# Second half of a branch merge: fp32 products as three fp32r products, with the weights' low parts made on GpSimd

## The chip, the cores and the metric
One core of one Trainium2 chip runs the whole kernel. The metric is the device time of one execution in microseconds (us), the median over runs. fp32r is float32 rounded to fewer bits, for TensorE; a "high part" is a value rounded to fp32r, a "low part" is what is left of it.

## The reference, cut to what matters
One layer of a hybrid backbone over 1024 latent tokens, width 1024. What the change touches is the merge of two branches:

```
def _merge(y_a, y_b, gate_logits, w_branch_a, w_branch_b, w_out):
    ga, gb = jnp.split(jax.nn.sigmoid(gate_logits), 2, axis=-1)
    return (ga * (y_a @ w_branch_a) + gb * (y_b @ w_branch_b)) @ w_out
...
    x_new = x + g1 * _merge(y_a, y_b, zx[..., OFF_G:], w_branch_a, w_branch_b, w_out)
    hx2 = _rms(x_new, norm2) * (1 + sc2) + sh2
    x_new = x_new + g2 * _expert_choice(hx2, router, w_gate, w_up, w_down)
```

y_a (from a long convolution) and y_b (from attention) are 1024 tokens by 512; w_branch_a and w_branch_b are 512 by 1024, w_out is 1024 by 1024. Before the merge stand the input projection, the attention and the long convolution; behind it the router, the choice of 128 tokens by each of 16 experts, and the experts' three matrices.

## The kernel before, in words
The kernel is a row of stages, each a block in which every engine has its own list of instructions and waits on semaphores; between stages all engines meet. The merge (`merge`, L1732 to L2080) is one such stage.

It works on transposed data: channels on the 128 partitions, tokens along the free axis. The inputs lie in SBUF when the stage starts: ya, yb, wa and wb, four chunks of 128 rows each, loaded (all but ya) during the convolution stage by `load_merge_input` (L1509). Sixteen branch jobs follow (L1857 to L1865, `m` in the list of jobs of L1787): job i has the half of the tokens h = i // 8 and the output chunk j = i % 8. In the first half a job has four fp32 products of 128x128 by 128x512 (w_a by y_a only); the part of y_b was computed in the stage before and comes back from DRAM as `mb_dram`. In the second half a job has eight, four for each branch. PSUM holds four jobs; job i waits until VectorE has read the bank of job i-4 (`read`).

VectorE follows with `gated(i)` (L1978): the gate by the first product (one operand in PSUM), the gate by the second (in the first half both operands in SBUF), and their sum; ScalarE rounds the sum to mT_hi (L1918); VectorE subtracts to get mT_lo (`merged_low`, L1995). The gates come from DRAM, two jobs ahead, on SP's queue (L1814), and behind the first two SP issues the load of w_out, 4 MB (L1819). ScalarE makes w_out's high parts (`out_high`, L1908) in the second half of the jobs, VectorE its low parts (`out_low`, L1973): two in front of each of the last four gated jobs for the left half of the columns, and eight behind the last job for the right half.

Then the output projection: `project(t, n)` (L1842) takes 128 tokens and 512 columns and issues 24 fp32r matmuls (8 chunks by three products, `three`, L220: high by high, high by low, low by high). The order is project(0,0), project(1,0), project(0,1), then tile by tile with the transposes and router products between (L1866 to L1899). VectorE multiplies by g1 (L2021), adds x (L2024), and the norm follows. SP loads the tiles of x (L1826) and stores the new ones (L1833), and after w_out's last low part it loads the first expert weights (L1828 to L1830). GpSimd has one memset in this stage (L1969).

Places in SBUF are shared by hand: wo_hi lies where ya and yb lie, wo_lo where wa and wb lie; a high or low part of w_out is written only when the branch products have read what it overwrites.

Of the kernel before, what the change touches and what calls it, by code (L numbers as in the profile page):

```python
# [20 lines left out]
P = 128  # L21
D = 1024
# [111 lines left out]
def build(nc, A, out):  # L134
    root = ExitStack()
    with root:
# [56 lines left out]
        with ExitStack() as s:  # L193
            sby, _ = scope(s)

            with ExitStack() as below:
                sbw, _ = scope(below)
                g["wo_hi"], g["wo_lo"] = (sbw(n, [P, KD, D], F32R) for n in ("wo_hi", "wo_lo"))
            g["ya"] = sby("ya", [P, NCH, L])
            with ExitStack() as below:  # L200
                sbw, _ = scope(below)
                g["yb"], g["wa"], g["wb"] = (sbw(n, [P, NCH, D]) for n in ("yb_in", "w_a", "w_b"))
            hyena(g, right, filters)
            g["late"] = root.enter_context(nc.sbuf_tensor("late", [P, L], F32, side="right"))
            g["affT"] = g["late"][0:AFF, 0:L // 2]

            with ExitStack() as below:
                g["mT_hi"], g["mT_lo"] = (below.enter_context(nc.sbuf_tensor(n, [P, KD, L], F32R, side="right"))
                                          for n in ("mT_hi", "mT_lo"))
            g["ring"] = root.enter_context(nc.sbuf_tensor("ring", [P, RAW, 2048], F32, side="right"))  # L210
            g["raw_in"] = [sem(f"raw_in{i}") for i in range(RAW)]
            merge(g)
# [1241 lines left out]
def convolve(g, KS, ti):  # L1454
# [9 lines left out]
    with ExitStack() as s:  # L1464
# [29 lines left out]
        with nc.Block() as block:  # L1494
            @block.sync
            def _(sp):
                def load_columns(j):
                    if j >= 2:
                        sp.wait_ge(branch_done, j - 1)
                    sp.dma_start(w2[:, j % 2], A["w_branch_b"][0][:, P * j:P * j + P].rearrange("(c p) n -> p c n", p=P))\  # L1500
                      .then_inc(w2_in[j % 2], 16)

                def load_gate(i):
                    if i:
                        sp.wait_ge(gated, 2 * i)
                    at = HY * (i // 2 + 1) + HC * (i % 2)
                    sp.dma_start(gate[:], g["z_dram"][at:at + HC, :].rearrange("(c p) t -> p c t", p=P)).then_inc(gate_in, 16)

                def load_merge_input(i, tile, src):  # L1509
                    sp.wait_ge(spec_ready, 2 * FC * (i + 1))  # L1510
                    sp.dma_start(tile[:], src.rearrange("(c p) n -> p c n", p=P)).then_inc(g["merge_in"], 16)

                load_columns(0)
                load_columns(1)
                sp.dma_start(y2[:], g["yb_dram"][:, 0:512].rearrange("(c p) t -> p c t", p=P)).then_inc(y2_in, 16)
                load_gate(0)
                load_columns(2)
                load_columns(3)
                load_columns(4)
                load_gate(1)  # L1520
                load_columns(5)
                load_merge_input(0, g["yb"], g["yb_dram"])
                load_gate(2)
                load_columns(6)
                load_merge_input(1, g["wa"], A["w_branch_a"][0])
                load_gate(3)
                load_columns(7)
                load_merge_input(2, g["wb"], A["w_branch_b"][0])

            @block.tensor  # L1530
            def _(pe):
# [200 lines left out]
def merge(g):  # L1732
# [10 lines left out]
    ident, mod, A2, ring = g["ident"], g["mod"], g["A2"], g["ring"]  # L1743
    ya, yb, wa, wb = g["ya"], g["yb"], g["wa"], g["wb"]
    mT_hi, mT_lo, wo_hi, wo_lo = g["mT_hi"], g["mT_lo"], g["wo_hi"], g["wo_lo"]
    wo = ring[:, 0:4].rearrange("p s n -> p (s n)").rearrange("p (k n) -> p k n", n=D)
    XB = 2
    with ExitStack() as s:
        sb, ps = g["scope"](s)
        sb("merge_inputs", [P, 3, NCH, D])  # L1750
        x_new = sb("x_new", [P, XB, D])
        step = sb("m_step", [P, D])
        mb = step[:].rearrange("p (b n) -> p b n", b=2)
        xn = sb("x_normed", [P, 2, D])
# [16 lines left out]
        job, read = sem("m_job"), sem("m_read")  # L1771
        mul, mt_ready, mt_hi, mt_lo = sem("m_mul"), sem("mt_ready"), sem("mt_hi"), sem("mt_lo")
        wo_high, wo_low = sem("wo_hi_ready"), sem("wo_lo_ready")
        xnew_ready, sq_ready = sem("xnew_ready"), sem("sq2_ready")
        v_step, rt_ready, xn_ready = sem("v2_step"), sem("rt2_ready"), sem("xn2_ready")
        h_ready = sem("h2_ready")
# [30 lines left out]
        with nc.Block() as block:  # L1807
            @block.sync
            def _(sp):
                for i in range(M):  # L1810
                    if i >= 2:
                        sp.wait_ge(mt_ready, i - 1)
                    h, j = divmod(i, KD)
                    sp.dma_start(gates[:, i % 2], g["gate_dram"][:, half(h)]  # L1814
                                 .rearrange("(v c p) t -> c p v t", v=2, p=P)[j]).then_inc(gates_in[i % 2], 16)
                    if h == 0:
                        sp.dma_start(mb[:, i % 2], g["mb_dram"][P * j:P * j + P, :]).then_inc(mb_in[i % 2], 16)
                    if i == 1:
                        sp.dma_start(wo, A["w_out"][0].rearrange("(c p) n -> p c n", p=P)).then_inc(o_in, 16)  # L1819
                        sp.dma_start(router[:], A["router"][0].rearrange("(c p) n -> p c n", p=P)).then_inc(r_in, 16)  # L1820
                for t in range(NT):
                    if t >= XB:
                        sp.wait_ge(x_stored[t % XB], 16 * (t // XB))
                        sp.wait_ge(xn_ready, t - XB + 1)
                        sp.wait_ge(job, n_job[("h", t - XB)])
                    sp.dma_start(x_new[:, t % XB], A["x"][0, P * t:P * t + P, :]).then_inc(xr_in[t % XB], 16)  # L1826
                    if t == 1:
                        sp.wait_ge(wo_low, 2 * NO)  # L1828
                        for i in range(4):
                            load_unit(sp, g, 0, i)  # L1830
# [10 lines left out]
            def _(pe):  # L1841
                def project(t, n):  # L1842

                    if t % 4 == 0 and n == 0:
                        pe.wait_ge(mt_lo, KD * (t // 4 + 1))
                    if t == 0:
                        pe.wait_ge(wo_low, NO * (n + 1))
                    if n == 0:
                        pe.wait_ge(read, M + 2 * (t - 1) if t >= 2 else M - 2 + t)
                    for k in range(KD):  # L1850
                        at = slice(P * t, P * t + P)
                        mm = three(pe, pj[:, t % 2, n], mT_hi[:, k, at], mT_lo[:, k, at],
                                   wo_hi[:, k, half(n)], wo_lo[:, k, half(n)], k == 0, k == KD - 1)
                    return mm

                pe.wait_ge(g["merge_in"], 48)
                for kind, t in jobs:  # L1857
                    if kind == "m":
                        h, j = divmod(t, KD)
                        if t >= 4:  # L1860
                            pe.wait_ge(read, t - 3)
                        for br, (w, y) in enumerate(((wa, ya), (wb, yb))[:h + 1]):
                            for c in range(NCH):
                                mm = pe.matmul(pj[:, t % 4, br], w[:, c, P * j:P * j + P], y[:, c, half(h)],
                                               start=c == 0, stop=c == NCH - 1)  # L1865
                    elif kind == "o":  # L1866
                        if t == 0:
                            project(0, 0)
# [38 lines left out]
            def _(act):  # L1907
                def out_high(k, n):  # L1908
                    act.activation(wo_hi[:, k, half(n)], wo[:, k, half(n)], ACT.Copy).then_inc(wo_high, 1)

                for i in range(M):
                    h, j = divmod(i, KD)
                    if i >= KD:
                        act.wait_ge(o_in, 16)
                        act.wait_ge(job, KD)
                        out_high(i - KD, 0)
                    act.wait_ge(mt_ready, i + 1)
                    act.activation(mT_hi[:, j, half(h)], ta[:, i % 2], ACT.Copy).then_inc(mt_hi, 1)  # L1918
                act.wait_ge(job, M)
                for k in range(NO):  # L1920
                    out_high(k, 1)

# [44 lines left out]
            @block.gpsimd  # L1967
            def _(pool):
                pool.memset(aff[:], 0.0).then_inc(aff_zero, 1)  # L1969

            @block.vector
            def _(dve):
# [22 lines left out]
                def merged_low(i):  # L1995
# [2 lines left out]
                    dve.tensor_tensor(mT_lo[:, j, half(h)], ta[:, i % 2], mT_hi[:, j, half(h)].bitcast(F32), ALU.subtract)\  # L1998
                       .then_inc(mt_lo, 1)

                for i in range(M):
                    if i >= KD + 4:
                        for k in range(2):
                            dve.wait_ge(job, KD + 4)
                            out_low(2 * (i - KD - 4) + k, 0)
                    gated(i)
                    merged_low(i)
                for k in range(NO):
                    out_low(k, 1)
# [442 lines left out]
```

## Time and profile before
| | us |
|---|---|
| median of 3 runs | 2245.38 |
| lowest and highest | 2242.11, 2246.43 |
| profiled execution, span from first to last instruction | 2242.3 |
| TensorE busy | 2145.9 (96%) |
| VectorE busy | 1655.7 (74%) |
| ScalarE busy | 1147.0 (51%) |
| GpSimd busy | 175.8 (8%) |

The profiled execution has its span on record, and no whole time of its own beside it; the median of the runs is 3.1 us longer than this span. PE is TensorE's matrix multiplication, PEld its weight load, DVE is VectorE, ACT ScalarE, POOL GpSimd, SP the engine that issues most DMAs (SPq its queue). TensorE's matmuls are pipelined, so the length of one record is more than the distance to the next; the pace is read from counts over a stretch. An fp32 matmul of 128x512 is two records. PEclk is the granted clock as a share of 2.4 GHz.

### The profile page before, as it was taken

The page shows a single profiled execution, that of the slowest core. Times are in us where ns is not written, and L with a number is a line of the kernel's source. Part 1 is how long each engine was busy: PE and PEld are TensorE (multiplying, and loading weights), DVE is VectorE, ACT ScalarE, POOL GpSimd, SP SyncE. Part 2 cuts the span into 40 slices and gives each one's busy share as a digit, 9 for nine tenths or more (in the row PEclk, how much of TensorE's full clock was granted, in tenths as well). Part 3 has the DMA queues.
Part 4 walks back from the last instruction along what each step waited for, and adds up shares of the span by engine and source line. Part 5 has one row for each costly group of instructions (what it writes and reads, how often), then busy time and mean ns, then how long its engine had stood idle before and what let it go on. Part 6 is the DMA issues. An engine that isn't in the chain of part 4 may idle for free.

```text
span 2242.3 us, 27253 instructions
## 1 busy us (share of the span) xinstructions
PE 2145.9 (96%) x10057; PEld 1695.6 (76%) x10057; DVE 1655.7 (74%) x1707; ACT 1147.0 (51%) x1201; POOL 175.8 (8%) x53
## 2 busy tenths in 40 slices
PE   7999999989999999999489999999999999999998
PEld 2998888856567776468468888888888888888886
DVE  3668754167654897553688889889889989898986
ACT  3521212165500220121257777777777777777775
POOL 0000000010000000000011011111011111011100
PEclk9999999999999999999789999999999999999999
DMA  8134454130020232643569999999999999999993
GB/s 305 61 98 163 142 178 141 47 118 13 17 80 6 70 131 91 221 168 113 197 236 364 393 394 380 380 378 380 399 391 380 378 382 384 396 387 380 380 378 121
DMA packets 183291, 539.38 MB, mean 241 GB/s; under 512 B 15231, under 2 KB 57355, under 8 KB 182708
## 3 DMA queue, kind: packets, MB, share of 16 engines
q1 hardware_dynamic: 172768, 506.72, 60.3%
q0 software_dynamic: 4752, 16.78, 2.9%
q10 hardware_dynamic: 5700, 14.90, 1.7%
q8 instruction: 48, 0.79, 0.1%
q14 instruction: 23, 0.19, 0.0%
HBM read 502.71 MB, written 35.65 MB: 240 GB/s over the span
## 4 chain that ended last, share of the span: by engine, by line
PE 49%; DVE 2%; DMA 0%; issue 0%; ACT 0%; POOL 0%; POOLq 0%
PE p_y L222 5%; PE p_y L224 5%; PE p_a L222 5%; PE p_a L224 5%; PE p_y L223 5%; PE p_a L223 5%; PE p_b L224 5%; PE p_b L223 5%; PE p_b L222 5%; PE p_t L2350 1%; PE p_t L2341 1%; DVE idx_rows L2305 1%; DVE late L2308 0%; DVE vals L2303 0%; DMA g1row<-xn_dram,idx_e 0%
## 5 line engine op out<-in xcount | busy, mean ns | idle before, releaser
L2246 DVE TENSOR_TENSOR r_lo<-ring,r_hi 128x2048 fp32r<-128x2048 f32 x384 | 865.8, 2287 | 62.8 <-ACT r_hi L2205 56.0
L2205 ACT ACTIVATE r_hi<-ring 128x2048 fp32r<-128x2048 f32 x384 | 731.0, 1915 | 154.4 <-PE p_b L224 74.7
L222 PE MATMUL p_y<-r_hi,a_hi 128*128 128x512 f32 x512 | 205.3, 401 | 0.0
L222 PE MATMUL p_a<-r_hi,x_hi 128*128 128x512 f32 x512 | 202.5, 396 | 1.0 <-DVE x_lo L2257 1.0
L224 PE MATMUL p_y<-r_hi,a_lo 128*128 128x512 f32 x512 | 200.0, 391 | 0.0
L224 PE MATMUL p_a<-r_hi,x_lo 128*128 128x512 f32 x512 | 199.8, 390 | 0.0
L223 PE MATMUL p_a<-r_lo,x_hi 128*128 128x512 f32 x512 | 199.2, 389 | 0.0
L223 PE MATMUL p_y<-r_lo,a_hi 128*128 128x512 f32 x512 | 199.2, 389 | 0.0
L222 PE MATMUL p_b<-r_hi,x_hi 128*128 128x512 f32 x512 | 199.2, 389 | 0.0
L223 PE MATMUL p_b<-r_lo,x_hi 128*128 128x512 f32 x512 | 199.2, 389 | 0.0
L224 PE MATMUL p_b<-r_hi,x_lo 128*128 128x512 f32 x512 | 199.2, 389 | 0.0
L222 PE MATMUL p_z<-h_hi,w_hi 128*128 128x512 f32 x448 | 177.0, 395 | 0.0
L224 PE MATMUL p_z<-h_hi,w_lo 128*128 128x512 f32 x448 | 174.5, 390 | 0.0
L223 PE MATMUL p_z<-h_lo,w_hi 128*128 128x512 f32 x448 | 174.4, 389 | 0.0
L2168 POOL DMA_INDIRECT g1row<-xn_dram,idx_e x16 | 121.4, 7587 | 58.5 <-issue 43.3
L2174 POOL DMA_INDIRECT out_x<-late,idx_s x17 | 45.3, 2666 | 914.6 <-DVE late L2296 914.6
L224 PEld LDWEIGHTS p_y<-r_hi,a_lo 128*128 128x128 f32 x512 | 96.1, 188 | 21.0
L224 PEld LDWEIGHTS p_a<-r_hi,x_lo 128*128 128x128 f32 x512 | 96.1, 188 | 20.5
L222 PEld LDWEIGHTS p_a<-r_hi,x_hi 128*128 128x128 f32 x512 | 96.2, 188 | 20.2 <-issue 1.4
L223 PEld LDWEIGHTS p_b<-r_lo,x_hi 128*128 128x128 f32 x512 | 96.1, 188 | 20.0
L222 PEld LDWEIGHTS p_b<-r_hi,x_hi 128*128 128x128 f32 x512 | 96.1, 188 | 20.0
L224 PEld LDWEIGHTS p_b<-r_hi,x_lo 128*128 128x128 f32 x512 | 96.1, 188 | 19.9
(319 smaller groups left out, 3577.7 us busy)
## 6 DMA issues: line engine op xcount, KB each, us to landing
ring<-in_w_gate SPq DMA_DIRECT2D x128, 1024.0 KB, 8.4
ring<-in_w_up SPq DMA_DIRECT2D x128, 1024.0 KB, 8.5
ring<-in_w_down SPq DMA_DIRECT2D x128, 1024.0 KB, 12.0
w_raw<-in_w_in SPq DMA_DIRECT2D x17, 1024.0 KB, 6.1
ada_rest<-in_ada_w SPq DMA_DIRECT2D x16, 1024.0 KB, 5.3
ada<-in_ada_w SPq DMA_DIRECT2D x8, 1024.0 KB, 15.3
gate_dram<-zs ACTq DMA_DIRECT2D x16, 512.0 KB, 2.6
x_normed<-gate_dram SPq DMA_DIRECT2D x16, 512.0 KB, 4.3
```

The source lines that it names most:

```text
L222: pe.matmul(out, a_hi, b_hi, start=start, stop=False)
L223: pe.matmul(out, a_hi, b_lo, start=False, stop=False)
L224: return pe.matmul(out, a_lo, b_hi, start=False, stop=stop)
L2168: pool.indirect_dma_start(out=xe[:], out_offset=None, in_=g["xn2_dram"][:, :], in_offset=bass.IndirectOffsetOnAxis(ap=idx_e[:, 0:1], axis=0))\
L2174: pool.indirect_dma_start(out=rows, in_=part, in_offset=None, out_offset=bass.IndirectOffsetOnAxis(ap=idx_s[:, at:at + 1], axis=0), comput ...
L2205: act.activation(r_hi[:, i % PARTS], ring[:, i % RAW], ACT.Copy).then_inc(hi_ready, 1)
L2246: dve.tensor_tensor(r_lo[:, i % PARTS], ring[:, i % RAW], r_hi[:, i % PARTS].bitcast(F32), ALU.subtract).then_inc(lo_ready, 1)
L2305: dve.max_index(rows[:, at], vals[:, at], aff).then_inc(found, 1)
L2341: mm = pe.transpose(p_t[:, bank, P * k:P * k + P], xe[:, P * (4 * q + k):P * (4 * q + k) + P], ident[:])
L2350: mm = pe.transpose(p_t[:, q % 2, P * k:P * k + P], au[:, q % 2, P * k:P * k + P], ident[:])
```

## The change
It does the branch products of the second half of the tokens (jobs 8 to 15) as three fp32r products each, as the projection does. The first half stays in fp32.

ScalarE makes the high parts of y_a and y_b for tokens 512 to 1023 (8 copies at the start of the stage) and those of the weights (two copies ahead of each of the first eight waits for mt_ready). VectorE makes the low parts of y (8 subtractions ahead of gated(0)). GpSimd makes the low parts of the weights (16 subtractions of 128x512, each after its high part; the one of w_a also after the first-half job that reads the same columns). Low parts lie in the place of the values they come from. The high parts lie where the second half of mT_hi and mT_lo will be (weights), where x_new will be (y_a), and in `late` and the unused first half of yb (y_b). So four things move: x is loaded after job 15; chunks 6 and 7 of w_out's left high parts are made after job 15; w_out's left low parts go behind `gated` in place of ahead of it; and the projection waits for them chunk by chunk. The convolution stage loads only the second half of y_b's tokens.

```
@@ load_merge_input, in the convolution stage @@
-                load_merge_input(0, g["yb"], g["yb_dram"])
+                load_merge_input(0, g["yb"][:, :, 512:L], g["yb_dram"][:, 512:L])
@@ merge: places @@
+    wa_hi, wb_hi = ([m[:, j, 512:L].rearrange("p (c n) -> p c n", c=NCH) for j in range(KD)] for m in (mT_hi, mT_lo))
+    wa_lo, wb_lo = g["wa_lo"], g["wb_lo"]
+        ya_lo = [g["ya_r"][:, c, second] for c in range(NCH)]
+        yb_lo = [g["yb_r"][:, c, second] for c in range(NCH)]
+        ya_hi = [x_parts[:, c] for c in range(NCH)]
+        yb_hi = [g["late_r"][:, 0], g["late_r"][:, 1], g["yb_r"][:, 2, 0:512], g["yb_r"][:, 3, 0:512]]
@@ sync @@
+                sp.wait_ge(job, M)
                 for t in range(NT):
@@ tensor, project @@
-                    if t == 0:
-                        pe.wait_ge(wo_low, NO * (n + 1))
+                    if t == 0 and n:
+                        pe.wait_ge(wo_low, 2 * NO)
                     for k in range(KD):
+                        if t == 0 and n == 0 and k in (0, 6, 7):
+                            pe.wait_ge(wo_low, max(k + 1, 6))
@@ tensor, branch jobs @@
-                        for br, (w, y) in enumerate(((wa, ya), (wb, yb))[:h + 1]):
+                        column = slice(P * j, P * j + P)
+                        for c in range(NCH if h == 0 else 0):
+                            mm = pe.matmul(pj[:, t % 4, 0], wa[:, c, column], ya[:, c, half(0)],
+                                           start=c == 0, stop=c == NCH - 1)
+                        branches = ((wa_hi[j], wa_lo, ya_hi, ya_lo), (wb_hi[j], wb_lo, yb_hi, yb_lo))
+                        for br, (w_hi, w_lo, y_hi, y_lo) in enumerate(branches if h else ()):
+                            if j == 0:
+                                pe.wait_ge(y_low, NCH * (br + 1))
+                            pe.wait_ge(w_low, 2 * j + br + 1)
                             for c in range(NCH):
-                                mm = pe.matmul(pj[:, t % 4, br], w[:, c, P * j:P * j + P], y[:, c, half(h)],
-                                               start=c == 0, stop=c == NCH - 1)
+                                mm = three(pe, pj[:, t % 4, br], w_hi[:, c], w_lo[:, c, column], y_hi[c], y_lo[c],
+                                           c == 0, c == NCH - 1)
@@ scalar @@
+                act.wait_ge(g["merge_in"], 48)
+                for y, y_hi in ((ya, ya_hi), (yb, yb_hi)):
+                    for c in range(NCH):
+                        act.activation(y_hi[c], y[:, c, second], ACT.Copy).then_inc(y_high, 1)
                 for i in range(M):
                     h, j = divmod(i, KD)
-                    if i >= KD:
+                    if i < KD:
+                        for w, w_hi in ((wa, wa_hi), (wb, wb_hi)):
+                            act.activation(w_hi[i], w[:, :, P * i:P * i + P], ACT.Copy).then_inc(w_high, 1)
+                    elif i < M - 2:
                         act.wait_ge(o_in, 16)
                         act.wait_ge(job, KD)
                         out_high(i - KD, 0)
+                    elif i == M - 1:
+                        act.wait_ge(job, M)
+                        out_high(6, 0)
+                        out_high(7, 0)
@@ gpsimd @@
+                for n in range(2 * KD):
+                    j, br = divmod(n, 2)
+                    w, w_hi, w_lo = ((wa, wa_hi, wa_lo), (wb, wb_hi, wb_lo))[br]
+                    column = slice(P * j, P * j + P)
+                    pool.wait_ge(w_high, n + 1)
+                    if br == 0:
+                        pool.wait_ge(job, j + 1)
+                    pool.tensor_tensor(w_lo[:, :, column], w[:, :, column], w_hi[j].bitcast(F32), ALU.subtract)\
+                        .then_inc(w_low, 1)
@@ vector @@
+                for b, (y, y_hi, y_lo) in enumerate(((ya, ya_hi, ya_lo), (yb, yb_hi, yb_lo))):
+                    for c in range(NCH):
+                        dve.wait_ge(y_high, NCH * b + c + 1)
+                        dve.tensor_tensor(y_lo[c], y[:, c, second], y_hi[c].bitcast(F32), ALU.subtract).then_inc(y_low, 1)
                 for i in range(M):
+                    gated(i)
                     if i >= KD + 4:
                         for k in range(2):
-                            dve.wait_ge(job, KD + 4)
                             out_low(2 * (i - KD - 4) + k, 0)
-                    gated(i)
                     merged_low(i)
```

## Rows read from the trace of the kernel before

**Rows 1.** The page, its first part: busy time of each engine.
```profile
PE 2145.9 (96%) x10057; PEld 1695.6 (76%) x10057; DVE 1655.7 (74%) x1707; ACT 1147.0 (51%) x1201; POOL 175.8 (8%) x53
```

**Rows 2.** Merge by stretches: first half, second half, projection's start; busy us (x instructions).
```profile
core 0: us, PE busy (x) PEld busy (x) DVE busy (x) ACT busy (x) POOL busy (x), PEclk, DMA share, GB/s
892.43:921.15 28.72, 28.68 (x63) 12.72 (x64) 12.20 (x19) 2.52 (x4) 0.26 (x1) 0.94 0.85 302
921.15:976.11 54.96, 54.96 (x130) 24.32 (x129) 32.13 (x50) 11.09 (x19) 0.00 (x0) 1.00 0.40 130
976.11:992.93 16.82, 16.82 (x73) 13.39 (x72) 7.69 (x13) 4.80 (x9) 0.00 (x0) 1.00 0.39 148
```

**Rows 3.** Branch products by tile p_m: ns min/median/max, first and last start.
```profile
L1864 PE MATMUL p_m<-ya,w_a x128: 592/592/1193, 892.5 to 972.7; 128*128 128x512 f32 x128
L1864 PE MATMUL p_m<-yb_in,w_b x64: 592/592/593, 925.0 to 976.1; 128*128 128x512 f32 x64
```

**Rows 4.** Timeline of the first half's end: start us, us, what.
```profile
897.77 0.69 DVE L1984 TENSOR_TENSOR h<-x_normed,p_m 128x512 f32<-128x512 f32 x1 [5.83 <-PE p_m L1864]
...
899.88 7.34 SPq L1814 DMA_DIRECT2D x_normed<-gate_dram  x1
...
912.55 0.69 DVE L1984 TENSOR_TENSOR h<-x_normed,p_m 128x512 f32<-128x512 f32 x1 [7.88 <-DMA x_normed<-gate_dram]
...
916.03 0.68 DVE L1984 TENSOR_TENSOR h<-x_normed,p_m 128x512 f32<-128x512 f32 x1
916.63 0.69 DVE L1990 TENSOR_TENSOR h<-x_normed,m_step 128x512 f32<-128x512 f32 x1
...
919.41 0.68 DVE L1984 TENSOR_TENSOR h<-x_normed,p_m 128x512 f32<-128x512 f32 x1
920.01 0.69 DVE L1990 TENSOR_TENSOR h<-x_normed,m_step 128x512 f32<-128x512 f32 x1
...
924.61 0.19 PEld L1864 LDWEIGHTS p_m<-yb_in,w_b 128*128 128x128 f32 x1 [0.24 <-issue]
...
932.98 0.68 DVE L1984 TENSOR_TENSOR h<-x_normed,p_m 128x512 f32<-128x512 f32 x1
```

**Rows 5.** Copies and subtractions of w_out: eight in a row, and the groups' means.
```profile
979.38 4.26 ACT L1909 ACTIVATE wo_hi<-ring 128x512 fp32r<-128x512 f32 x8
...
980.12 4.90 DVE L1975 TENSOR_TENSOR wo_lo<-ring,wo_hi 128x512 fp32r<-128x512 f32 x8
...
L1918 ACT ACTIVATE mT_hi<-h 128x512 fp32r<-128x512 f32 x16 | 10.1, 629 | 84.5 <-DVE h L1993 84.5
L1909 ACT ACTIVATE wo_hi<-ring 128x512 fp32r<-128x512 f32 x16 | 9.2, 616 | 0.0
```

**Rows 6.** GpSimd's two-input operation, by its line: ns min/median/max.
```profile
L974 POOL TENSOR_TENSOR fpm<-fout x2: 2349/2362/2375, 463.3 to 465.6; 128x1024 f32<-128x1024 f32 x2
```

**Rows 7.** GpSimd's indirect DMAs and VectorE's subtractions in the expert stage.
```profile
1135.13 1.14 POOL L2168 DMA_INDIRECT g1row<-xn_dram,idx_e  x1 [39.06 <-issue]
...
L2168 POOL DMA_INDIRECT g1row<-xn_dram,idx_e x16: 1141/7957/8845, 1135.1 to 2105.8; - x16
...
L2246 DVE TENSOR_TENSOR r_lo<-ring,r_hi x384: 2278/2285/2295, 1139.7 to 2223.9; 128x2048 fp32r<-128x2048 f32 x192
```

**Rows 8.** Timeline of the hand-over to the projection.
```profile
976.11 0.19 PEld L222 LDWEIGHTS p_m<-wo_hi,mT_hi 128*128 128x128 f32 x1 [0.24 <-issue]
...
984.93 0.29 DVE L2012 TENSOR_TENSOR router_scaled<-router_w,A 128x128 f32<-128x128 f32 x1
```

**Rows 9.** Loads of x on SP's queue, their time to landing, and the first use.
```profile
965.51 0.94 SPq L1826 DMA_DIRECT2D x_new<-in_x  x2
...
x_new<-in_x SPq DMA_DIRECT2D x8, 512.0 KB, 4.5
...
993.53 0.69 DVE L2021 TENSOR_TENSOR m_step<-p_m,g1row 128x512 f32<-128x512 f32 x1 [8.31 <-PE p_m L224]
```

**Rows 10.** Stretches around the clock's dip and in the choice of tokens; columns as rows 2.
```profile
896.00:900.00 4.00, 4.00 (x11) 1.75 (x10) 1.98 (x3) 0.11 (x1) 0.00 (x0) 1.00 0.92 342
...
1014.00:1018.00 4.00, 4.00 (x20) 3.52 (x20) 2.18 (x10) 2.00 (x5) 0.00 (x0) 0.64 0.32 33
1018.00:1022.00 4.00, 4.00 (x17) 3.20 (x17) 0.00 (x0) 0.00 (x0) 0.00 (x0) 0.93 0.91 356
...
1100.00:1110.00 10.00, 0.00 (x0) 0.00 (x0) 9.52 (x23) 0.95 (x1) 0.00 (x0) 0.50 1.03 415
```

More of the change, by code:

```diff
@@ L198, in build @@
                 g["wo_hi"], g["wo_lo"] = (sbw(n, [P, KD, D], F32R) for n in ("wo_hi", "wo_lo"))
+            with ExitStack() as below:
+                sbw, _ = scope(below)
+                g["ya_r"], g["yb_r"], g["wa_lo"], g["wb_lo"] = (sbw(n, [P, NCH, D], F32R)
+                                                                for n in ("ya_parts", "yb_parts", "w_a_lo", "w_b_lo"))
             g["ya"] = sby("ya", [P, NCH, L])
@@ L203, in build @@
             hyena(g, right, filters)
+            with ExitStack() as below:
+                g["late_r"] = below.enter_context(nc.sbuf_tensor("late_parts", [P, 2, L // 2], F32R, side="right"))
             g["late"] = root.enter_context(nc.sbuf_tensor("late", [P, L], F32, side="right"))
@@ L1510, in load_merge_input @@
                     sp.wait_ge(spec_ready, 2 * FC * (i + 1))
-                    sp.dma_start(tile[:], src.rearrange("(c p) n -> p c n", p=P)).then_inc(g["merge_in"], 16)
+                    sp.dma_start(tile, src.rearrange("(c p) n -> p c n", p=P)).then_inc(g["merge_in"], 16)
                 load_columns(0)
@@ L1521, in _ @@
                 load_columns(5)
-                load_merge_input(0, g["yb"], g["yb_dram"])
+                load_merge_input(0, g["yb"][:, :, 512:L], g["yb_dram"][:, 512:L])
                 load_gate(2)
                 load_columns(6)
-                load_merge_input(1, g["wa"], A["w_branch_a"][0])
+                load_merge_input(1, g["wa"][:], A["w_branch_a"][0])
                 load_gate(3)
                 load_columns(7)
-                load_merge_input(2, g["wb"], A["w_branch_b"][0])
+                load_merge_input(2, g["wb"][:], A["w_branch_b"][0])
             @block.tensor
@@ L1750, in merge @@
         sb("merge_inputs", [P, 3, NCH, D])
+        with ExitStack() as below:
+            x_parts = g["scope"](below)[0]("x_parts", [P, NCH, 512], F32R)
         x_new = sb("x_new", [P, XB, D])
+        second = slice(512, L)
+        ya_lo = [g["ya_r"][:, c, second] for c in range(NCH)]
+        yb_lo = [g["yb_r"][:, c, second] for c in range(NCH)]
+        ya_hi = [x_parts[:, c] for c in range(NCH)]
+        yb_hi = [g["late_r"][:, 0], g["late_r"][:, 1], g["yb_r"][:, 2, 0:512], g["yb_r"][:, 3, 0:512]]
         step = sb("m_step", [P, D])
@@ L1773, in merge @@
         wo_high, wo_low = sem("wo_hi_ready"), sem("wo_lo_ready")
+        y_high, y_low = sem("y_hi_ready"), sem("y_lo_ready")
+        w_high, w_low = sem("branch_hi_ready"), sem("branch_lo_ready")
         xnew_ready, sq_ready = sem("xnew_ready"), sem("sq2_ready")
@@ L1916, in _ @@
                         out_high(i - KD, 0)
+                    elif i == M - 1:
+                        act.wait_ge(job, M)
+                        out_high(6, 0)
+                        out_high(7, 0)
                     act.wait_ge(mt_ready, i + 1)
                     act.activation(mT_hi[:, j, half(h)], ta[:, i % 2], ACT.Copy).then_inc(mt_hi, 1)
-                act.wait_ge(job, M)
                 for k in range(NO):
```

## The prediction

> **What bounds the kernel now.** I read the engine totals first, then the merge in stretches, then VectorE's order of time inside it, and last the places where the end of the merge is handed on. TensorE is busy 96% of the span [rows 1], so the first question is what its own work in the changed stage costs. The sixteen branch jobs run without a gap: eight for the first half of the tokens (four fp32 products each), eight for the second half (eight each), and then the output projection [rows 2]. Each fp32 product is two matmul records, 128 records for w_a and 64 for w_b [rows 3]. The second half takes 54.96 us for 128 records, 0.429 us a record and 0.859 us a product; in the projection 72 fp32r matmuls take 16.82 us, 0.2336 us each, and three of them 0.701 us [rows 2].
>
> VectorE has room in the second half (32.1 us of 55) but not in the first. There it waits for gates that stand behind the 4 MB load of w_out: the gates of job 2, due at 899.88, take 7.34 us to be issued, and gated(2) starts at 912.55. From then one job costs VectorE 3.38 us (916.03 to 919.41), as much as TensorE's 3.43 us for four products [rows 4]. TensorE has four banks, so job i needs the second multiply of gated(i-4). Job 8, the first of the second half, begins 8 records before the load at 924.61, at 921.18; the multiply that frees its bank starts at 920.01 and is out by 920.7. So the margin is some 0.45 us there, and by the same rows as little at jobs 6 and 7.
>
> **The change, part by part.** The range of my sum hangs on two terms, the products and what GpSimd does to VectorE.
>
> *Products.* 64 products at 0.859 - 0.701 = 0.158 us: 10.1 us less on TensorE. It has no gap there, so all of it is on the path if nothing else becomes late. A second-half job falls from 6.87 to 5.61 us. The first half keeps its fp32 form.
>
> *High parts on ScalarE.* Eight copies of y (0.53 us each at the pace of eight like copies in a row, 0.62 for one alone [rows 5]) start with the stage and end some 4.3 to 5 us later. The sixteen of w go in pairs ahead of each wait for mt_ready, 1.2 us in a cycle of 3.4 in which ScalarE now has one copy of 0.63 us. They are hidden by VectorE's three operations on the next job; without that cover they would cost 1.2 us a cycle.
>
> *Low parts of y on VectorE.* Eight subtractions, paced at 0.61 us like those of w_out [rows 5], end near 892.4 + 0.6 + 8 x 0.61 = 897.9 us, and gated(0) started at 897.77 [rows 4]. Behind them waits the whole job loop, but gated(2) waits for its gates until 912.55 in any case. Nothing. If the gates came early, it would cost at most 5 us of a lead that TensorE's four banks half hide.
>
> *Low parts of w on GpSimd.* The nearest row is a two-input operation on 128x1024 in 2.36 us [rows 6]; for 128x512 the bounds are 1.18 us (half the elements) and 2.36 us (no gain from the smaller size). I take 1.2: two of them in a row leave almost no fixed part between them. Sixteen are 19 us, spread over TensorE's first 29 us; the last pair may start when job 7 is done (921.2) and is needed by job 15 near 960. So GpSimd is not late by itself. What counts is what it does beside VectorE. In this trace no VectorE operation with two SBUF inputs stands beside a GpSimd one that reads SBUF. The nearest rows are the indirect DMAs: 1.14 us for the one issued while VectorE idled, 7.96 us in the median beside the back-to-back r_lo subtractions, which keep their 2.28 to 2.30 us [rows 7]. So the two engines can hold each other up, and bounds for VectorE are nothing (as r_lo) and the whole of GpSimd's time. I take the whole, less what falls beside VectorE's waits and its first multiply, which reads PSUM and one SBUF tile. Per job: 2 x 1.2 = 2.4 us, less 0.6 for the first multiply and 0.1 of gaps, 1.7 us more. The Trainium skill, SBUF — State Buffer, section Who interferes with whom, says so in words: an operation of VectorE with two SBUF inputs and a GpSimd operation that reads SBUF exclude each other, and the later one stands still until the earlier has ended. By that rule the sum is the one I give; by the r_lo row alone it would be 10.1 us. No run here shows that pair yet.
>
> Where it falls: w_hi of job j is made after mT_hi of job j-1, so GpSimd's pair for j = 0 to 2 is over before 912.55, and those for j = 3 to 7 run beside gated(3) to gated(7). The pair for job 3 starts near 915.95, and gated(3)'s second multiply (916.63) is held to 917.15 or 918.35, as GpSimd's second operation goes behind it or before it. Job 7 of TensorE waits up to 1.3 us, and job 8 waits for gated(4)'s: 920.7 + 1.7 + 0.5 to 1.7 = 922.9 to 924.1 against 921.18, so 1.7 to 2.9 us, and I take 2.3. Job 9 needs gated(5)'s by 924.1 + 3.4 + 0.5 to 1.7 = 928.0 to 929.2 and comes at 928.5 to 929.7: TensorE at 5.61 us a job now outruns the delay. VectorE falls back 5 x 1.7 = 8.5 us by gated(8) (932.98 before, 941.5 after [rows 4]), then takes 3.4 us a job, and from gated(12) some 4.0 (the wait for ScalarE is now covered by the two w_out subtractions), 967.0 for gated(15): TensorE ends job 15 at 921.18 + 2.3 + 44.9 = 968.4. It has caught up, by a little over 1 us.
>
> *Hand-over.* Two of the w_out low parts now stand after gated(15), for their place holds y_b's high part. Before, the last subtraction ended 8.9 us after the projection began (976.11, and 984.93 for the operation behind it [rows 8]). Now it is 1.25 us more behind that job, less 0.65 of wait covered: 9.5 us. The first 48 matmuls of the projection cover 11.2 us, so 1.7 us are left and the cost is nothing; uncovered it would be 1 us. The first wait of the projection, six low parts, is met by gated(14)'s pair, near 966.
>
> *Loads of x.* They move behind job 15 on SP's queue, because their place holds y_a's high part. Before, both were issued at 965.51 and used at 993.53 + 0.7 [rows 9]; now they go near 968.4 and land 4.5 us later, while the first use is 17 us off. Behind them on SP stands the expert weights' first load, which waits for the last w_out low part anyway. Nothing. The halved load of y_b (1 MB less) lies far ahead in the Hyena stage: nothing.
>
> *Clock.* The granted clock is 1.00 from 896 on, with a dip to 0.64 and 0.93 in 1014 to 1022, right after the small router matmuls [rows 10]. At 0.36 x 4 + 0.07 x 4 = 1.7 us it is the size of what a shifted start can gain or lose; I take nothing and keep 1.7 us both ways. Later, TensorE idles through the choice of the experts' tokens (0 us of 10 in 1100 to 1110 [rows 10]), so all behind the merge shifts whole.
>
> Sum: -10.1 + 2.3 = -7.8 us. Against the profiled execution's span of 2242.3 that is 2234.5; 3.1 us lie between the span and the median of the three runs, 2245.38, which gives 2237.6.
>
> **Rivals.** *No interference.* If VectorE is not held at all, TensorE keeps its 10.1 us: 2235.3. For it: r_lo's unchanged length. Against it: the sevenfold indirect DMA. A short lock, shared in another order, lies between this and my case.
>
> *GpSimd holds VectorE until it is the bound.* With c us more per job, VectorE frees job 11's bank at 930.9 + 5c, and five jobs of 5.61 us later the projection begins at 959 + 5c. It equals 976.1 at c = 3.4, that is at 2.05 us per GpSimd operation. With the upper bound of 2.36 us, c is 4.0: 979, 3 us slower, 2248.3; with a clock dip more, 2250. For it: the strided columns of w, which no row has. Against it: two back-to-back operations of 1024 elements at 2.35 and 2.37 show little that would not shrink with the size.
>
> *A middle case.* c = 2.7 (1.7 us per operation) gives 972.5, a gain of 3.6: 2241.8, inside the 0.2% (4.5 us) that a measurement of this kernel can tell from no change.
>
> *The products do not get cheaper.* If three fp32r matmuls cost here what one fp32 product does (0.286 us a matmul), nothing is gained and the 2.3 us of delay stay: 2247.7. Nothing in rows 2 speaks for it: the same shapes with the same weight loads run at 0.2336.
>
> **How the numbers follow.** My case 0.50, no interference 0.22, the middle case 0.14, GpSimd as the bound 0.10, no cheaper products 0.04. The forecast is my case, 2237.6. The range reaches to the no-interference case with a gain of the clock, 2233.6, and up over the middle case to 2243.0. Faster by over 0.2% means below 2240.9: my case and the first rival, 0.72; within it the middle case and half of the last two, 0.21, since 2247.7 and 2248.3 lie within 4.5 us of the median; slower by more, with the clock against it, their other half, 0.07.
>
> **What would show it.** Right: 192 records of fp32r matmuls at 0.2336 us in the second half, w_lo operations near 1.2 us or stretched, VectorE's second multiply or add of jobs 3 to 7 longer or late by about 1.7 us a job, job 8 some 2 us after its granted time and no wait of TensorE after it. Wrong: w_lo above 2 us, a projection that begins later than 971 or that stops before its third run of 24, a wait on the last w_out low part, or a dip of the clock elsewhere.

## The result and the profile after

The changed kernel takes 2233.52 us in the median of four runs (2230.49 to 2236.2), against 2245.41 us: a ratio of 0.9947, interval 0.9934 to 0.9961. The forecast was 2237.6 us in a range from 2233.6. The sign and the mechanism came as forecast; the gain was sized too small, and the median lies 0.1 us under the range. The same kernel run again gave 2234.38 us in five runs, ratio 0.9951 (0.9937 to 0.9965), which lies inside it.

The page of the changed kernel, its span and first part, beside [rows 1]:

```profile
span 2232.3 us, 27436 instructions
PE 2134.9 (96%) x10121; PEld 1707.7 (76%) x10121; DVE 1669.2 (75%) x1715; ACT 1159.1 (52%) x1225; POOL 199.2 (9%) x69
```

The span is 10.0 us shorter, and TensorE's busy time falls by 11.0. The merge in the stretches of [rows 2] (first half, second half, start of the projection; the columns are those of rows 2):

```profile
892.19:921.87 29.68, 29.14 (x64) 12.68 (x64) 21.21 (x26) 11.99 (x22) 13.60 (x11) 0.95 0.82 292
921.87:966.10 44.23, 44.22 (x192) 35.98 (x193) 35.79 (x48) 13.21 (x23) 10.08 (x7) 1.00 0.43 138
966.10:982.92 16.82, 16.82 (x74) 13.54 (x73) 8.80 (x15) 5.96 (x11) 0.00 (x0) 1.00 0.57 201
```

By these bounds the second half went from 54.96 to 44.23 us, the first half is 0.96 us longer, and in it TensorE's total is 0.5 short of the stretch. The bounds are not at like places, though. Before the change both ends of the second half lie at a weight load, 0.4 us ahead of the matmuls (job 8's first matmul started at 921.60); afterwards it begins at job 8's first matmul and ends at the projection's first weight load, 0.2 us ahead of that matmul (966.30). From matmul to matmul the second half took 54.9 us (128 records, 0.429 us apart) and takes 966.30 - 921.88 = 44.4, 10.5 less; the first half took 29.1 us and takes 29.65, 0.5 more. Below I call "the merge" the time from the first branch matmul to the first weight load of the projection: 976.11 - 892.47 = 83.6 us before, 966.10 - 892.23 = 73.9 after. From there to the end of the span it is 1266.2 us in both kernels, so the profiles' whole gain was made in the merge, but for 0.2 us of an earlier start.

TensorE's timeline, its only wait inside the merge (in brackets the idle time ahead of an instruction, and who ended it):

```profile
892.23 29.14 PE L1884 MATMUL p_m<-ya,w_a 128*128 128x512 f32 x64 [2.92 <-PEq L1500]
921.88 0.50 PE L228 MATMUL p_m<-x_parts,mT_hi 128*128 128x512 f32 x1 [0.51 <-DVE h L2037]
922.21 0.40 PE L229 MATMUL p_m<-ya_parts,mT_hi 128*128 128x512 f32 x1
```

L2037 is gated(4)'s second multiply: job 8 waits for its bank, where the prediction had it. VectorE's and GpSimd's timelines around it, VectorE's to be laid beside [rows 4]:

```profile
911.80 0.69 DVE L2031 TENSOR_TENSOR h<-x_normed,p_m 128x512 f32<-128x512 f32 x1 [4.54 <-DMA x_normed<-gate_dram]
...
915.29 0.68 DVE L2031 TENSOR_TENSOR h<-x_normed,p_m 128x512 f32<-128x512 f32 x1
915.88 1.18 DVE L2037 TENSOR_TENSOR h<-x_normed,m_step 128x512 f32<-128x512 f32 x1
917.17 1.57 DVE L2040 TENSOR_TENSOR h<-h 128x512 f32<-128x512 f32 x1
919.43 0.69 DVE L2045 TENSOR_TENSOR mT_lo<-h,mT_hi 128x512 fp32r<-128x512 f32 x1 [0.69 <-ACT mT_hi L1957]
920.04 0.68 DVE L2031 TENSOR_TENSOR h<-x_normed,p_m 128x512 f32<-128x512 f32 x1
920.64 1.18 DVE L2037 TENSOR_TENSOR h<-x_normed,m_step 128x512 f32<-128x512 f32 x1
```
```profile
915.24 1.27 POOL L2015 TENSOR_TENSOR w_a_lo<-w_a,mT_hi 128x512 fp32r<-128x512 f32 x1 [5.61 <-ACT mT_hi L1947]
916.47 1.72 POOL L2015 TENSOR_TENSOR w_b_lo<-w_b,mT_lo 128x512 fp32r<-128x512 f32 x1
```

Read them together. The multiply issued at 915.88 takes 1.18 in place of 0.69 us: it stood until GpSimd's first operation ended at 916.51. GpSimd's second one was issued at 916.47 and takes 1.72 in place of 1.27: it stood until the multiply ended at 917.06. The add issued at 917.17 ends at 918.74, after GpSimd's end at 918.19. The engines take turns. The first multiply (PSUM and one SBUF tile) and the subtraction at 919.43 keep their length: the first has a GpSimd operation beside it and only one operand in SBUF, the second has no GpSimd operation beside it. VectorE's job takes 920.04 - 915.29 = 4.75 us in place of 3.38. This agrees with the rule quoted from the Trainium skill, SBUF — State Buffer, section Who interferes with whom.

The hand-over, beside [rows 8] and [rows 9]:

```profile
966.50 0.82 SPq L1844 DMA_DIRECT2D x_new<-in_x  x2
...
970.31 4.90 DVE L2022 TENSOR_TENSOR wo_lo<-ring,wo_hi 128x512 fp32r<-128x512 f32 x8
975.13 0.28 DVE L2062 TENSOR_TENSOR router_scaled<-router_w,A 128x128 f32<-128x128 f32 x1
...
984.03 0.69 DVE L2074 TENSOR_TENSOR x_new<-x_new,m_step 128x512 f32<-128x512 f32 x1
```

The last w_out low part is done at 970.31 + 4.90, 9.1 us into the projection, whose first 48 matmuls last 11.2 us; TensorE does not stop. The loads of x leave at 966.50, and their first use is the addition at 984.03.

### The profile page after: what moved, and what is told of

Its sections match the earlier page's. It is cut to its first block, busy times and chain, and to the rows that moved or that the text cites. A ratio compares the mean times of both kernels' runs of the same rounds, so it can differ in the third digit from the quotient of the medians.

```text
span 2232.3 us, 27436 instructions
## 1 busy us (share of the span) xinstructions
PE 2134.9 (96%) x10121; PEld 1707.7 (76%) x10121; DVE 1669.2 (75%) x1715; ACT 1159.1 (52%) x1225; POOL 199.2 (9%) x69
## 4 chain that ended last, share of the span: by engine, by line
PE 49%; DVE 2%; DMA 0%; issue 0%; ACT 0%; POOL 0%; POOLq 0%
PE p_y L228 5%; PE p_y L230 5%; PE p_a L228 5%; PE p_a L230 5%; PE p_y L229 5%; PE p_a L229 5%; PE p_b L228 5%; PE p_b L230 5%; PE p_b L229 5%; PE p_t L2400 1%; PE p_t L2391 1%; DVE idx_rows L2355 1%; DVE late L2358 0%; DVE vals L2353 0%; DMA g1row<-xn_dram,idx_e 0%
## 6 DMA issues: line engine op xcount, KB each, us to landing
ring<-in_w_down SPq DMA_DIRECT2D x128, 1024.0 KB, 11.9
```

## The experiments

All times of the merge are read as above; a kernel's own median is given beside it where it was timed.

**The changed kernel again.**

> The changed kernel once more, to size the spread between executions. The merge's length is the time from the first branch matmul to the first weight load of the projection: 83.6 us before the change, 73.9 after it. My theory: the length repeats to 0.1 us, and what differs between executions (2230.5 to 2236.2 us) lies behind the merge, where the granted clock differs; the ratio to the kernel before is 0.9953 (10.0 to 10.5 us) with a lasting spread of 2 us. Rival: the change gains another 2 us somewhere that one profile did not show, and the ratio stays at 0.9947 or below.

Merge 968.7 - 894.75 = 73.95 us, again one wait, of 0.55 us, at job 8. The length repeats. But this merge began 2.5 us later than in the first profile, so the spread lies ahead of it, not behind it as I had written; the stretches in which it arises are shown further down.

**GpSimd makes no low parts.**

```
-                for n in range(2 * KD): ... pool.tensor_tensor(w_lo ...)
-                            pe.wait_ge(w_low, 2 * j + br + 1)
+                            pe.wait_ge(w_high, 2 * j + br + 1)
-  three(pe, pj[:, t % 4, br], w_hi[:, c], w_lo[:, c, column], y_hi[c], y_lo[c], ...)
+  three(pe, pj[:, t % 4, br], w_hi[:, c], w_hi[:, c], y_hi[c], y_lo[c], ...)
```

> GpSimd makes no low parts; the third product of each three reads the high part in place of the low one (so the low parts of the weights are left out, with as many matmuls). My theory, that the pair of GpSimd operations is what stretches VectorE's job from 3.38 to 4.75 us and holds TensorE at job 8: the cycle returns to 3.38 us, the wait of about 0.9 us at job 8 goes, the merge is 73.0 us, the kernel 0.9 us faster than the changed one. Rival, that ScalarE's extra copies or the crowded SBUF stretch it: the cycle stays near 4.75 and the merge at 73.9.

```profile
915.92 0.68 DVE L2022 TENSOR_TENSOR h<-x_normed,p_m 128x512 f32<-128x512 f32 x1
916.52 0.69 DVE L2028 TENSOR_TENSOR h<-x_normed,m_step 128x512 f32<-128x512 f32 x1
917.31 0.69 DVE L2031 TENSOR_TENSOR h<-h 128x512 f32<-128x512 f32 x1
...
919.31 0.68 DVE L2022 TENSOR_TENSOR h<-x_normed,p_m 128x512 f32<-128x512 f32 x1
```

VectorE's job is back at 3.39 us, TensorE waits nowhere, the merge is 966.22 - 892.76 = 73.5 us. ScalarE's extra copies were all still there, so they stretch nothing. 0.5 us of the expected 0.9 is missing. Most of it is pace: the fp32r matmuls stood 0.2327 us apart here, with the high part in the place of the low one, and 0.2308 in the changed kernel, 0.4 us over 191 of them. The median, 2233.85 us, can't show either.

**GpSimd only writes.**

```
-   pool.tensor_tensor(w_lo[:, :, column], w[:, :, column], w_hi[j].bitcast(F32), ALU.subtract)
+   pool.memset(w_lo[:, :, column].bitcast(F32), 0.0)
```

> Each of GpSimd's sixteen subtractions becomes a memset of the same 128x512 output with the same waits (so the low parts of the weights are zero). If what excludes VectorE is GpSimd's reading of SBUF: VectorE's job takes 3.38 us, no wait at job 8, merge 73.0 us, and no memset is stretched. If any GpSimd operation excludes it: VectorE's second multiply and add are held by a part of the memsets' length, some 0.3 us a job or more.

```profile
914.03 0.53 POOL L2015 MEMSET w_b_lo<- 128x512 f32 x1
914.17 0.69 DVE L2036 TENSOR_TENSOR h<-x_normed,m_step 128x512 f32<-128x512 f32 x1
```

The memset runs in the middle of the two-input multiply, and neither is longer; all sixteen take 0.53 us, the job 3.38, the merge 963.5 - 890.45 = 73.1 us, with no wait of TensorE. So GpSimd at work, writing to SBUF, does not exclude VectorE's second SBUF operand. That its reading does is what fits, but the memset is also another and a shorter operation; none that reads a single tile was run. The merge is 0.8 us shorter than the changed kernel's, close to the 0.9 that I had expected of the exclusion's absence; its one execution took 2231.16 us.

**GpSimd's pairs later.**

```
                     pool.wait_ge(w_high, n + 1)
+                    if j >= 3 and br == 0:
+                        pool.wait_ge(mt_ready, j + 2)
```

> GpSimd's pairs for chunks 3 to 7 also wait for the sum of job j+1 (mt_ready j+2), so that they run beside gated(5) to gated(9), past the point where TensorE has no margin. My theory: the same stretch of 1.4 us a pair, but no wait of TensorE: merge 73.0 us, 0.9 us faster than the changed kernel. Rival: the delay only moves, TensorE waits at a later job for a bank or for a low part, and the merge stays at 73.9 or grows.

```profile
891.80:920.36 28.56, 28.53 (x64) 12.66 (x65) 19.79 (x27) 11.99 (x22) 8.81 (x7) 0.95 0.87 305
920.36:964.90 44.54, 44.54 (x193) 36.02 (x192) 34.75 (x48) 13.22 (x23) 15.01 (x10) 1.00 0.44 137
```

No wait of TensorE, merge 73.1 us. GpSimd's sum is as long as before (23.8 us of busy time in the two stretches, 23.7 in the changed kernel), and it still holds VectorE (4.49 us a job), but where there is room. The median is 2232.97 us (0.9942, 0.9929 to 0.9956), level with the load of w_out in four parts below (2232.94); from the changed kernel (0.9947, 0.9934 to 0.9961) the timing can tell neither.

**The load of w_out later.** `if i == 1:` before the loads of w_out and of the router becomes `if i == 5:`.

> The load of w_out and of the router goes behind the gates of job 5 in place of job 1. My theory: the wait of 4.5 us for the gates of job 2 goes, VectorE runs ahead of TensorE at 4.75 us a job, and TensorE has no wait at job 8: merge 73.0 us. Against it, the gates of jobs 6 and 7 now stand behind the load and may come later than 930; then TensorE waits at job 10, and the merge is 74 to 76 us. Rival, that the margin at job 8 is set by the sum of GpSimd's pairs and not by the gates: merge stays 73.9.

```profile
923.00 0.69 DVE L2045 TENSOR_TENSOR mT_lo<-h,mT_hi 128x512 fp32r<-128x512 f32 x1 [0.70 <-ACT mT_hi L1957]
931.11 0.69 DVE L2031 TENSOR_TENSOR h<-x_normed,p_m 128x512 f32<-128x512 f32 x1 [7.42 <-DMA x_normed<-gate_dram]
```
```profile
889.50:918.10 28.60, 28.53 (x64) 12.66 (x65) 23.97 (x27) 12.57 (x24) 15.16 (x11) 0.95 0.55 180
...
929.00:934.00 5.00, 2.22 (x9) 1.51 (x8) 2.08 (x4) 0.68 (x2) 0.00 (x0) 0.94 0.62 231
934.00:940.00 6.00, 6.00 (x22) 4.73 (x22) 5.20 (x7) 2.15 (x4) 2.98 (x2) 0.77 0.40 109
```

The wait at job 8 is gone (28.60 us for the first half, beside VectorE's jobs of 4.75 us), so the gates' place did set that margin. But the same 4 MB now stand in front of the gates of job 6: VectorE waits 7.42 us, TensorE 2.78 at job 10, and after that idle time its clock is granted at 0.77 for 6 us, another 1.4 us. Merge 967.23 - 889.57 = 77.7 us, longer than I had allowed; median 2239.38 (0.9979, 0.9970 to 0.9988).

**The load of w_out in four parts.**

```
-                    if i == 1:
-                        sp.dma_start(wo, ...).then_inc(o_in, 16)
+                    if 1 <= i <= 4:
+                        part = slice(2 * i - 2, 2 * i)
+                        sp.dma_start(wo[:, part], ...[:, part]).then_inc(o_in, 16)
+                    if i == 4:
                         sp.dma_start(router[:], ...)
-                        act.wait_ge(o_in, 16)
+                        act.wait_ge(o_in, 64)
```

> The load of w_out goes in four parts of 1 MB, behind the gates of jobs 1 to 4; GpSimd's low parts stay as in the changed kernel. If the margin at job 8 comes from the gates of job 2 standing behind the whole load: no wait of VectorE for gates above 1 us, no wait of TensorE at job 8 although VectorE's jobs still take 4.75 us, first half 28.6 us, merge 73.1 us against 73.9, and none of the 2.8 us wait and the dip of the clock that the late load brought. Rival, that GpSimd's pairs alone set it: the wait at job 8 stays.

VectorE waits 0.55 and 0.57 us for gates, TensorE nowhere: first half 28.6 us, merge 965.4 - 892.35 = 73.1, median 2232.94 (0.9945, 0.9931 to 0.9959). The wait at job 8 needed both, the late gates and GpSimd's pairs; taking away either is enough.

**VectorE makes the weights' low parts.**

```
                     merged_low(i)
+                    for br in range(2 if i < KD else 0):
+                        w, w_hi, w_lo = ((wa, wa_hi, wa_lo), (wb, wb_hi, wb_lo))[br]
+                        column = slice(P * i, P * i + P)
+                        dve.wait_ge(w_high, 2 * i + br + 1)
+                        dve.tensor_tensor(w_lo[:, :, column], w[:, :, column], w_hi[i].bitcast(F32), ALU.subtract)...
```

> VectorE makes the sixteen low parts itself, a pair behind each of the first eight merged_low; GpSimd makes none. My theory: a pair costs VectorE 1.22 us, so a job takes 4.60 us, less than the 4.75 beside GpSimd; but the pair of job 2 now stands ahead of gated(3), where GpSimd's was over before, so gated(4)'s second multiply ends near 922.3 in place of 921.8, and the merge is 74.4 us, 0.5 longer than after the change. Rival, that GpSimd truly takes work off VectorE: a job here takes 5 us or more, and the merge is above 75 us.

```profile
917.21 0.69 DVE L2053 TENSOR_TENSOR w_a_lo<-w_a,mT_hi 128x512 fp32r<-128x512 f32 x1
917.81 0.69 DVE L2053 TENSOR_TENSOR w_b_lo<-w_b,mT_lo 128x512 fp32r<-128x512 f32 x1
918.42 0.68 DVE L2022 TENSOR_TENSOR h<-x_normed,p_m 128x512 f32<-128x512 f32 x1
...
923.00 0.68 DVE L2022 TENSOR_TENSOR h<-x_normed,p_m 128x512 f32<-128x512 f32 x1
```

A job takes 4.58 us, less than the 4.75 beside GpSimd. The merge is 968.5 - 893.90 = 74.6 us (expected 74.4), with a wait of 0.88 us at job 8; median 2235.92 (0.9959, 0.9946 to 0.9972). So GpSimd takes nothing off VectorE while VectorE is busy with two-input work: making the pair costs it 1.2 us, standing by while GpSimd makes it costs 1.37. GpSimd's help is worth something only while VectorE waits, as it did before 911.80.

**VectorE makes them, late.** As above, with the pairs behind jobs 0, 1, 4 (chunk 2) and 5 to 9 (chunks 3 to 7).

> VectorE makes all low parts of the weights, those of chunks 0 and 1 behind their jobs, that of chunk 2 behind job 4 and those of chunks 3 to 7 behind jobs 5 to 9; GpSimd makes none. My theory: a pair costs 1.22 us of VectorE against 1.11 us beside GpSimd in the late order, TensorE waits nowhere, and the merge is 73.1 us, as with GpSimd late: so what matters is where the pairs stand, not which engine makes them. Rival, that VectorE falls behind at the end of the merge: the projection begins late or waits for the last w_out low part, and the merge is 74 us or more.

Merge 965.7 - 892.60 = 73.1 us, no wait of TensorE, nothing late at the end; median 2235.67 (0.9959, 0.9944 to 0.9974). The profile says as good as GpSimd late. The medians of the two are 2.7 us apart and their intervals overlap, so the times do not decide between them.

**One fp32 product of the high parts.**

```
-  mm = three(pe, pj[:, t % 4, br], w_hi[:, c], w_lo[:, c, column], y_hi[c], y_lo[c], ...)
+  mm = pe.matmul(pj[:, t % 4, br], w_hi[:, c].bitcast(F32), y_hi[c].bitcast(F32), ...)
```

> All high and low parts are made and waited for, but each product of the second half is one fp32 matmul of the two high parts (so the products with low parts are left out). It shows what the products alone are worth. My theory: second half 54.96 us in place of 44.23, merge 84.6 us, the kernel 0.9 us slower than the one before the change. Rival, that part of the gain came from the moved x loads, the order of the w_out low parts or the halved load of y_b: the merge is clearly shorter than 84.6, or the rest of the kernel shorter than before.

```profile
894.90:924.66 29.76, 29.17 (x64) 12.69 (x64) 21.21 (x26) 11.98 (x22) 13.55 (x11) 0.95 0.82 291
924.66:979.30 54.64, 54.63 (x128) 24.26 (x129) 35.88 (x48) 13.17 (x23) 9.91 (x7) 1.00 0.35 112
```

Merge 84.4 us, and the kernel is no faster than the one before: 2245.89 us, ratio 1.0000 (0.9990 to 1.0009). All parts, moves and the halved load are in it; only the products are back in fp32. So the whole gain is the products', and the rest of the change costs 84.35 - 83.64 = 0.7 us of merge, with TensorE waiting 0.58 us at job 8.

**Every subtraction of GpSimd twice.**

```
+                    for again in range(2):
+                        if again: pool.wait_ge(w_low, 2 * n + 1)
+                        pool.tensor_tensor(w_lo[...], w_lo[...] if again else w[...], w_hi[j]..., ALU.subtract)...
-                            pe.wait_ge(w_low, 2 * j + br + 1)
+                            pe.wait_ge(w_low, 4 * j + 2 * br + 2)
```

> GpSimd does every subtraction twice, the second on the result of the first (so the low parts are wrong by one high part). It shows how far the exclusion can go. My theory: four GpSimd operations of 1.27 us alone meet three exclusive operations of VectorE in a job, a job takes about 5.9 us, jobs 9 to 11 of TensorE go at that pace, and the merge is 76.2 us, still 7 us shorter than before the change. Rival, as in the prediction's slower case, that GpSimd's whole time comes on top: 4 x 1.27 - 0.7 = 4.4 us more a job, a projection that begins near 959 + 5 x 4.4 = 981 by the blind formula, a merge of 88 us, slower than before the change.

```profile
926.37 0.68 DVE L2034 TENSOR_TENSOR h<-x_normed,p_m 128x512 f32<-128x512 f32 x1
926.96 1.18 DVE L2040 TENSOR_TENSOR h<-x_normed,m_step 128x512 f32<-128x512 f32 x1
928.25 1.60 DVE L2043 TENSOR_TENSOR h<-h 128x512 f32<-128x512 f32 x1
930.55 1.01 DVE L2048 TENSOR_TENSOR mT_lo<-h,mT_hi 128x512 fp32r<-128x512 f32 x1 [0.70 <-ACT mT_hi L1957]
931.48 0.67 DVE L2034 TENSOR_TENSOR h<-x_normed,p_m 128x512 f32<-128x512 f32 x1
```

GpSimd never rests here, yet the job takes 5.1 us: each of the three two-input operations waits for at most what is left of one GpSimd operation (0.5, 0.9 and 0.3 us), and the rest runs beside ScalarE's copy and the first multiply. For the job both numbers that I gave were too high (5.9, and 4.4 us on top of 3.38), the rival's far more. The merge is 968.6 - 891.81 = 76.8 us (expected 76.2), with TensorE waiting 0.52, 1.32 and, at the first w_out low parts, 0.96 us; the rival's 88 us is far off. Its one execution took 2236.32 us.

## Why the prediction was right or wrong

**Products** (10.1 us forecast). Right in kind; 10.5 us came, from matmul to matmul (10.7 by the bounds of the stretches). In the branch jobs the fp32r matmuls behind the first stand (966.30 - 922.21)/191 = 0.2308 us apart, from the second of job 8 to the first of the projection. I took the pace of another stage as exact, 0.2336, and 192 matmuls turn 0.0028 us into 0.5. The 0.2336 was itself close by luck: its 16.82 us held the starts of 71 matmuls and not 72, and the first of them takes 0.64 us to the next; between 977.00 and 991.00 sixty took 0.2333 us each. The fp32 experiment shows that nothing else of the change gains anything.

**GpSimd beside VectorE** (2.3 us forecast, 0.8 measured). This is the step that failed, in its size. The merge is 73.9 us with the wait and 73.1 in each of the four runs without it that keep the matmuls and their pace (memset, GpSimd late, w_out in four parts, VectorE late). The first half grew by 0.5 only: its first four matmuls, which stand up to 0.99 us apart at the start of the stage, took 3.22 us in place of 3.38, and 0.1 of the delay falls behind job 8's first start. The mechanism, the engines' exclusion, the job (8) and the VectorE operation that TensorE waits for were right; three numbers were not. The stretch is 1.37 us a job and not 1.7. I took a pair as 2.4 us with 0.7 of cover. Alone it is 2 x 1.27 = 2.54 us, and 1.17 of it is covered: 0.64 by the first multiply (915.24 to 915.88), 0.11 by the gap between the second multiply and the add, and the rest because a held operation takes 0.14 us less from its release to its end than it takes alone (0.55 for 0.69 twice on VectorE, 1.13 for 1.27 on GpSimd). The second multiply of gated(4) is held 0.5 us, the lowest end of my 0.5 to 1.7, because the engines take turns and GpSimd's second operation goes behind it; I took the middle. And the gates of job 2 came at 911.80, not 912.55, 0.5 us earlier against the start of the stage; why, no run shows. Together: 920.7 - 0.75 + 1.37 + 0.5 = 921.82, which is when that multiply ended (920.64 + 1.18).

The forecast was 4.1 us too long: 1.5 are this term, 0.4 the products, and 2.2 lie outside the merge (below). Without these 2.2 us the median would have been 2235.7, inside the range.

**What was costed at nothing.** Right each time: ScalarE's copies (VectorE's job is 3.39 us with them and without GpSimd), the low parts of y (gated(0) at 897.69, against 897.77 before), the moved loads of x, and the w_out low parts (done 9.1 us into the projection, forecast 9.5). VectorE had caught up by the end of the merge.

**From the span to the median.** The two terms as measured, 10.5 - 0.8 = 9.7 us (the merge: 83.6 - 73.9), would have given 2235.7 from the median before, and the two profiled spans are 10.0 us apart. The first four runs showed 11.9 us, the next five 10.4. The last 2 us fit a matter of which executions were drawn: the shortest of the first four (2230.49 us) had a mean granted clock of 0.984, the longest (2236.2) one of 0.980. In the profiles, stretches ahead of the merge differ. This is the one from 725 to 760, in the convolution stage, of the changed kernel and of the one with the later w_out load:

```profile
725.00:760.00 35.00, 32.44 (x123) 23.43 (x124) 21.30 (x26) 10.61 (x19) 0.00 (x0) 0.90 0.31 105
```
```profile
725.00:760.00 35.00, 32.24 (x135) 23.77 (x136) 24.12 (x27) 11.51 (x20) 0.00 (x0) 1.00 0.35 120
```

The same code runs in both. Where the clock is granted at 0.90 fewer instructions fit in the same time, and the merge began at 892.2; with 1.00 it began at 889.6. It is not the only such stretch. The changed kernel's second profile has 0.90 there too, and its merge began at 894.75. It differs from the first in the stretch from 450 to 475 (first profile, then second), and in that from 600 to 625 (1.00, then 0.93):

```profile
450.00:475.00 25.00, 16.73 (x100) 12.01 (x98) 16.65 (x35) 18.17 (x40) 7.02 (x8) 1.00 0.70 254
```
```profile
450.00:475.00 25.00, 19.11 (x100) 14.26 (x98) 14.93 (x31) 16.79 (x36) 7.02 (x8) 0.86 0.70 254
```

Over the eleven profiles of the changed kernel and its variants the merge began between 889.6 and 894.9. I had looked for the clock's chance behind the merge (1.7 us around the router's matmuls) and allowed no more in the range; the larger one, 5 us, lay ahead of it. The profile before the change has 0.90 in 725 to 760 as well, and its merge began at 892.5. Whether the change shifts those chances at all stays open.

**The rivals.** No interference fell: the exclusion is plain in the rows. The trace's gain came close to its 10.1 us for another reason, a small delay and a faster pace. GpSimd as the bound fell by its price: one operation takes 1.27 us alone, far from the 2.05 it needed, and the doubled GpSimd shows that the formula behind it, with GpSimd's whole time on top, does not hold. The middle case needed 1.7 us an operation and fell with it; the case of products no cheaper needed 0.286 us a matmul, against 0.2308. What stretches the indirect DMAs of [rows 7], on which the argument for interference leaned, no run here shows.

## What to carry to other kernels

Two engines that exclude each other operation by operation cost each other, in every profile here, at most the rest of one operation per turn, not the whole time of the other; count turns, not sums. GpSimd beside a VectorE that works on two SBUF tiles saves nothing (1.37 us of standing by against 1.2 us of work), so give it what falls into VectorE's waits, or put the work past the point where the margin is small. A big load in front of small urgent ones on a queue sets such a point; cutting it in four removed it, delaying it moved it.

## What the runs showed of the hardware that was not expected

A GpSimd memset (0.53 us) runs inside a two-input VectorE operation with no effect on either, while a subtraction that reads SBUF excludes it. The Trainium skill, SBUF — State Buffer, section Who interferes with whom, states this.

Going from fp32 to fp32r matmuls costs no time, though the records look like it. Where TensorE had not waited, the first fp32r record starts with the last fp32 one and is longer. GpSimd late, then before the change, at the head of the projection:

```profile
920.36 0.80 PE L228 MATMUL p_m<-x_parts,mT_hi 128*128 128x512 f32 x1
921.00 0.39 PE L229 MATMUL p_m<-ya_parts,mT_hi 128*128 128x512 f32 x1
```
```profile
976.13 0.80 PE L222 MATMUL p_m<-wo_hi,mT_hi 128*128 128x512 f32 x1
976.77 0.39 PE L223 MATMUL p_m<-wo_lo,mT_hi 128*128 128x512 f32 x1
```

The last fp32 record starts at 920.33 and at 976.10, so from it to the second fp32r record it is 0.67 us both times, to 0.01 us the pace of one fp32 record (0.429) and one fp32r (0.231). In the changed kernel, with its wait at job 8, the same distance is 922.21 - 920.77 = 1.44 us. So the wait cost 0.8 us, which is what came back where it was removed, although the profile shows 0.51 us as idle.

fp32r matmuls of one shape ran 0.2308 us apart in the branch jobs, 0.2333 in the projection, and (966.45 - 922.00)/191 = 0.2327 with the high part of the weights in the place of the low one. No run here tells why.
